# Products of a triangular inverse on 32 columns in place of 64, in one decoder layer on one core

## The chip, the cores and the metric

The kernel runs on one NeuronCore of a Trainium2 chip. The metric is the device time of one execution in microseconds (us); of a set of runs the median is given. Engines are called by the profile's names: PE multiplies matrices (PEld is its loading of weights, the stationary operand), DVE is the vector engine, ACT the scalar engine, POOL the GpSimd engine, SP the queue that issues most transfers.

## What is computed

One layer of a hybrid decoder, on 256 tokens of width 2048, float32 throughout:

```
x = x + 0.5 * swiglu(rmsnorm(x), w1)                       # 2048 -> 5632 -> 2048
z = rmsnorm(x) @ w_in                                      # attention part | RWKV-7 part
x = x + concat(attention(z), rwkv7(z)) @ w_out
x = x + 0.5 * swiglu(rmsnorm(x), w2)
x = x + sigmoid(rmsnorm(x) @ w_ple_gate) * (p @ w_ple_proj)
```

The RWKV-7 part has 16 heads of 64 columns, each with a 64 x 64 state that every token changes:

```
def step(state, inp):
    r_t, w_t, k_t, v_t, kk_t, a_t = inp
    sa = einsum('bhvk,bhk->bhv', state, -kk_t)
    state = state * w_t + sa[..., None] * (kk_t * a_t) + v_t[..., None] * k_t
    return state, einsum('bhvk,bhk->bhv', state, r_t)
```

## The kernel before

The feed-forward parts and the projections stream float32 weights from memory in blocks of 1 MB. ACT rounds a block (L335), DVE takes the rest (L344), and PE forms three products of each tile (L358 to L360). They take the time up to some 1000 us and from 1161 us on.

Between them lies the RWKV stage. It doesn't step through the tokens: the 256 tokens are cut into 4 chunks of 64, and within a chunk the recurrence is one triangular system of 64 unknowns for each head. The 16 heads go in 4 groups (`GROUPS`, index `r`) of 4 heads, so a group has 16 systems. Two systems, of the two chunks in a tile of 128 tokens, stand one above the other on partitions 0 to 63 and 64 to 127; so the tiles `AB` (the systems' matrices), `X` (the inverse so far), `XT` (its transpose) and `Q` have 8 entries `s` of 64 columns, and each entry takes two calls of `matmul`, one for each half of the partitions (`c` in 0, 1). Both calls use a 64 x 64 corner of PE's array, and the two corners lie on its diagonal.

The inverse is built by doubling, in six levels with blocks of l = 1, 2, 4, 8, 16, 32. Level 1 is a predicated copy (L1613). The other five (`INV`, index `n` from 0 to 4) each make two products. The first is AB times XT, into a PSUM bank; ACT copies from it into `Q` the columns that belong to even blocks of l columns (L1493). The second is X times Q (at the last level Q times X), into another bank; DVE takes from it, by `copy_predicated` with a constant mask, the even blocks' columns into `XT` (L1633; at the last level the odd blocks' columns into `X`, L1631), and turns 32 x 32 blocks of `XT` over into `X` (`flip`, L1620). So of each 64-column product only 32 columns are read. `Q`'s other columns are zero from the start.

The 8 entries go in halves `h` of 4, so that ACT and DVE can work on one half while PE works on the other: PE does both halves of the first product, then both of the second, each half waiting on its own semaphore count (`low_ready`, `inv_qs` with `up_ready`). The order of every engine is written out by hand. Between the levels stand other works: on PE the gates of the next group (`pe_gates`, L1247 to L1264) and the transposes of the previous group's output (`pe_out`, L1424); on DVE the next group's preparation (`front`, L1552 to L1582) during levels 2 to 4, the previous group's normalisation (`out_centre`, `out_spread`, L1690 to L1699) in levels 0 and 1, and in the last group splits of weight blocks (L344). POOL ends the normalisation (L1059, L1160), and `pe_out` waits for it. After the inverse the chunk states follow in `pe_state` (L1363 to L1401).

`matmul(out, a, b)` holds `a` in the array and streams `b` through it. In the trace a float32 call leaves two records of loading and two of multiplying, so a half of 8 calls has 16 records and both halves have 32.

Of the kernel before, what the change touches and what calls it, by code (L numbers as in the profile page):

```python
# [16 lines left out]
P = 128  # L17
# [14 lines left out]
CHUNK = 64  # L32
# [85 lines left out]
def hybrid_layer(nc, table, w, out):  # L118
    where = constant_table()[1]
    ctx = ExitStack()  # L120
    with ctx:
# [10 lines left out]
        def sb(name, shape, dt=F32, at=None):  # L132

            if at is None:
                at = base[0]
                base[0] += -(-size(shape) // 64) * 64
                assert base[0] <= limit, (name, base[0] - limit)
            return nc.alloc_sbuf_tensor_at(name, shape, dt, offset=at)
# [21 lines left out]
        def const(name):  # L160
            a, n = where[name]
            return con[:, a:a + n]
# [6 lines left out]
        h = sb("h", [P, TT, COLS])  # L169
# [52 lines left out]
        X = sb("X", [P, 8, CHUNK], at=HT)  # L222
        Q = sb("Q", [P, 8, CHUNK], at=HT + 2048)
        pvst = sb("pvst", [P, TT, COLS], at=HT + 4096)
        XT = sb("XT", [P, 8, CHUNK])
        AB0 = base[0]
        AB = sb("AB", [P, 8, 2 * CHUNK])
# [36 lines left out]
        PS = ctx.enter_context(nc.psum_tensor("PS", [P, 8, COLS], F32))  # L264
        ident = const("ident")

        def sem(name):
            return ctx.enter_context(nc.semaphore(name))
# [34 lines left out]
        low_ready, up_ready = sem("low_ready"), sem("up_ready")  # L303
# [910 lines left out]
        INV = LEVELS[1:]  # L1214
        EARLY, LATER = (0, 1), (2, 3, 4)

        def odd_cols(a, l):

            return a.rearrange("p s (b two l) -> p s b two l", two=2, l=l)[:, :, :, 1, :]

        def even_cols(a, l):
            return a.rearrange("p s (b two l) -> p s b two l", two=2, l=l)[:, :, :, 0, :]

        HALF_BANKS = ((6, 4), (7, 5))
# [3 lines left out]
        def ahead(r, n):  # L1228

            if r == GROUPS - 1:  # L1230
                return ()
            return {2: (0,), 3: (1, 2), 4: (3, 4)}.get(n, ()) if r == 0 else (n + 1,) if n + 1 < GATE_PARTS else ()
# [5 lines left out]
        def pe_gates(pe, r, part):  # L1238

            mine, wl3 = fr(r).sigw, WL[r % 2]  # L1240
            if part == 0:
                if r == 0:
                    pe.wait_ge(ho_ready, 2)
                pe.wait_ge(*loaded(r))
                for k in range(2):
                    for t in range(TT):
                        ins = nc.tensor.matmul(PS[:, gate_bank(r, k), t * 256:(t + 1) * 256], lora_t[0:65, k, t * P:(t + 1) * P],  # L1247
                                               wl3[0:65, k, :], start=True, stop=True)
            for t in range(TT):
                one, two = PS[:, gate_bank(r, 0), t * 256:(t + 1) * 256], PS[:, gate_bank(r, 1), t * 256:(t + 1) * 256]  # L1250
                if part == 1:
                    pe.wait_ge(gates_ready, 2 * r + 1)
                    ins = nc.tensor.matmul(one, const("cum_in"), mine[:, t, :], start=True, stop=True)
                elif part == 2:
                    pe.wait_ge(gates_ready, 2 * r + 2)
                    ins = nc.tensor.matmul(two, const("cum_ex"), mine[:, t, :], start=True, stop=True)
                elif part == 3:
                    pe.wait_ge(exps_ready, 5 * r + 2)
                    for pr in range(2):
                        ins = nc.tensor.matmul(PS[:, gate_bank(r, 0), pr * 4 + 2 * t:pr * 4 + 2 * t + 2],  # L1260
                                               mine[:, t, pr * P:(pr + 1) * P], const("cum_all"), start=True, stop=True)
                elif part == 4:
                    pe.wait_ge(exps_ready, 5 * r + 3)
                    ins = nc.tensor.matmul(two, lora_t[:, 2, t * P:(t + 1) * P], wl3[:, 2, :], start=True, stop=True)  # L1264
            ins.then_inc(lora_out, 1)

        def systems(lo=0, hi=8):

            return [(s, s // 4, (s // 2) % 2, s % 2) for s in range(lo, hi)]
# [18 lines left out]
        def half(k):  # L1288
            return slice(k * CHUNK, (k + 1) * CHUNK)
# [25 lines left out]
        def by_chunks(bank, s, out_col, a, a_cols, b, start=True, stop=True):  # L1315

            for c in range(2):
                ins = nc.tensor.matmul(PS[half(c), bank, out_col:out_col + CHUNK], a[half(c), s, a_cols], b[half(c)],  # L1318
                                       start=start, stop=stop)
            return ins  # L1320

        def pe_inverse(pe, r, levels):

            for n in levels:
                last = n == len(INV) - 1
                for h in range(2):
                    pe.wait_ge(low_ready, 9 * r + (1 if n == 0 else 2 * n + h))
                    for s, *_ in systems(4 * h, 4 * h + 4):
                        ins = by_chunks(HALF_BANKS[h][0], s, (s % 4) * CHUNK, AB, half(0), XT[:, s, :])
                    ins.then_inc(inv_q, 1)  # L1330
                for part in ahead(r, n):
                    pe_gates(pe, r + 1, part)
                for h in range(2):
                    pe.wait_ge(inv_qs, 10 * r + 2 * n + h + 1)
                    pe.wait_ge(up_ready, 11 * r + (1 if n == 0 else 2 * n + h))
                    for s, *_ in systems(4 * h, 4 * h + 4):
                        a, b = (Q, X) if last else (X, Q)
                        ins = by_chunks(HALF_BANKS[h][1], s, (s % 4) * CHUNK, a, half(0), b[:, s, :])
                    ins.then_inc(inv_x, 1)

        def own_tokens(pe, t):
# [146 lines left out]
        def act_inverse(act, r, levels):  # L1488
            for n in levels:
                l = INV[n]  # L1490
                for h in range(2):
                    act.wait_ge(inv_q, 10 * r + 2 * n + h + 1)
                    nc.scalar.activation(even_cols(Q[:, 4 * h:4 * h + 4, :], l),  # L1493
                                         even_cols(PS[:, HALF_BANKS[h][0], 0:256].rearrange("p (s c) -> p s c", s=4), l),
                                         ACT.Copy).then_inc(inv_qs, 1)
                for part in ahead(r, n):
                    act_gates(act, r + 1, part)
                if r == GROUPS - 1 and n in LATER[:2]:
                    act.wait_ge(front_ready, 4 * GROUPS)
                    split_hi(act, WOUT + n - LATER[0])  # L1500
# [45 lines left out]
        def dve_rwkv(dve):  # L1546
            v = nc.vector
# [44 lines left out]
            def joins(l, k, n):  # L1592
                return const(f"join{l}")[:, 32 * k:32 * k + 32].rearrange("p (b l) -> p b l", l=l).unsqueeze(1).broadcast_to(
                    [P, n, 32 // l, l]).bitcast(U32)
# [27 lines left out]
            def inverse(r, levels, nxt, before, heads=False):  # L1622
                for n in levels:
                    l, last = INV[n], n == len(INV) - 1
                    for h in range(2):
                        dve.wait_ge(inv_x, 10 * r + 2 * n + h + 1)
                        v.memset(gate_step[:, h:h + 1], 0.0)
                        src = PS[:, HALF_BANKS[h][1], 0:256].rearrange("p (s c) -> p s c", s=4)
                        mine = slice(4 * h, 4 * h + 4)
                        if last:  # L1630
                            v.copy_predicated(odd_cols(X[:, mine, :], l), joins(l, 0, 4), odd_cols(src, l)).then_inc(up_ready, 1)  # L1631
                        else:
                            v.copy_predicated(even_cols(XT[:, mine, :], l), joins(l, 1, 4), even_cols(src, l)).then_inc(low_ready, 1)  # L1633
                            dve.wait_ge(low_ready, 9 * r + 2 * n + h + 2)
                            flip(X, XT, 4 * h, 4 * h + 4).then_inc(up_ready, 1)
                        if nxt is not None:
                            front(nxt, 2 * (n - LATER[0]) + h)
                        elif n in LATER[:2] and h == 1:
                            dve.wait_ge(front_ready, 4 * GROUPS)
                            split_lo(dve, WOUT + n - LATER[0])  # L1640
                        if heads and h == 1:
                            dve_heads_lo(dve, n)
                        if before is not None and (n, h) == (0, 1):
                            out_centre(before)
                        if before is not None and (n, h) == (1, 1):
                            out_spread(before)
# [327 lines left out]
```

## Time and profile before

| what | value |
|---|---|
| median of 3 runs | 2094.85 us (2089.59 to 2095.48) |
| the profiled execution | 2094.18 us, span 2092.4 us |
| PE busy | 2032.9 us, 97% of the span |
| DVE, ACT, POOL busy | 55%, 41%, 7% |
| mean granted clock of PE | 0.991 of full |
| 996 to 1161 us: PE busy, granted clock | 130.26 of 165 us, 0.92 |

The span goes from the first to the last instruction. A granted clock of 1.00 is PE's upper level, 2.4 GHz, and 0.50 its lower one, 1.2 GHz; a value between them is a mean over a stretch that has both. Busy time counts a matmul from its start to its modelled end, and matmuls overlap, so a busy PE need not be at its peak rate.

### The profile page before, as it was taken

How to read it: one execution, taken by the hardware profiler on the slowest of the kernel's cores; microseconds unless marked ns; L12 is line 12 of the kernel's file. 1: busy time of each engine (PE TensorE's matmuls, PEld its weight loads, DVE VectorE, ACT ScalarE, POOL GpSimd, SP SyncE). 2: the span in 40 equal slices, each digit the busy share in tenths (PEclk: the TensorE clock that was granted, in tenths of full speed). 3: DMA queues.
4: the chain of work that ended last, by engine and by line, in shares of the span. 5: the costliest groups of instructions: out<-in, count | busy, mean ns of one | idle time of the engine just before them, and what ended most of it. 6: DMA issues, size and time to landing. Idle time of an engine off the chain costs nothing.

```text
span 2092.4 us, 27658 instructions
## 1 busy us (share of the span) xinstructions
PE 2032.9 (97%) x11448; PEld 1696.6 (81%) x11448; DVE 1154.4 (55%) x1027; ACT 861.3 (41%) x833; POOL 148.6 (7%) x117
## 2 busy tenths in 40 slices
PE   8999999999999998999787999999999999999999
PEld 6888888888888887888676887888888888888887
DVE  4455545555555554767677444455554555455564
ACT  5343334333433346853332336333333434343353
POOL 0000000000000000354324100000000000000000
PEclk9999999999999999999998999999999999999999
DMA  7555555655556546766301455555565555555554
GB/s 256 192 190 195 186 190 191 192 188 187 194 184 197 183 146 201 215 189 196 100 24 56 138 186 170 188 190 191 185 196 189 192 193 188 187 194 191 191 180 142
DMA packets 190050, 373.62 MB, mean 179 GB/s; under 512 B 7111, under 2 KB 16963, under 8 KB 189981
## 3 DMA queue, kind: packets, MB, share of 16 engines
q1 hardware_dynamic: 186300, 361.47, 53.5%
q0 software_dynamic: 3680, 11.15, 1.8%
q8 instruction: 53, 0.87, 0.2%
q14 instruction: 17, 0.13, 0.0%
HBM read 363.94 MB, written 5.52 MB: 177 GB/s over the span
## 4 chain that ended last, share of the span: by engine, by line
PE 92%; DVE 5%; issue 2%; DMA 1%; ACT 0%; POOL 0%; SPq 0%; DVEq 0%; POOLq 0%
PE PS L358 29%; PE PS L360 29%; PE PS L359 29%; PE PS L415 1%; PE PS L1318 1%; PE PS L379 1%; DVE wlo L344 1%; DVE X L1620 1%; DVE XT L1633 0%; DMA x_resid<-in_x 0%; PE PS L1282 0%; DVE AB L1606 0%; DMA raw<-in_w_q_b 0%; PE PS L1401 0%; DVE AK L1606 0%
## 5 line engine op out<-in xcount | busy, mean ns | idle before, releaser
L344 DVE TENSOR_TENSOR wlo<-raw,whi 128x2048 fp32r<-128x2048 f32 (+1 forms) x338 | 777.7, 2301 | 763.3 <-PE PS L360 759.5
L335 ACT ACTIVATE whi<-raw 128x2048 fp32r<-128x2048 f32 (+1 forms) x338 | 642.9, 1903 | 996.7 <-PE PS L360 986.1
L358 PE MATMUL PS<-whi,xT_hi 128*128 128x512 f32 (+2 forms) x1936 | 753.0, 389 | 0.0
L360 PE MATMUL PS<-whi,xT_lo 128*128 128x512 f32 (+2 forms) x1936 | 748.2, 386 | 0.0
L359 PE MATMUL PS<-wlo,xT_hi 128*128 128x512 f32 (+2 forms) x1936 | 748.0, 386 | 0.0
L360 PEld LDWEIGHTS PS<-whi,xT_lo 128*128 128x128 f32 x1936 | 363.8, 188 | 73.6
L358 PEld LDWEIGHTS PS<-whi,xT_hi 128*128 128x128 f32 x1936 | 364.0, 188 | 72.0 <-issue 0.4
L359 PEld LDWEIGHTS PS<-wlo,xT_hi 128*128 128x128 f32 x1936 | 364.0, 188 | 72.0
L358 PE MATMUL PS<-whi,hT_hi 128*128 128x512 f32 x680 | 264.8, 389 | 2.6 <-DVE wlo L344 2.6
L360 PE MATMUL PS<-whi,hT_lo 128*128 128x512 f32 x680 | 264.6, 389 | 0.0
L359 PE MATMUL PS<-wlo,hT_hi 128*128 128x512 f32 x680 | 264.5, 389 | 0.0
L358 PEld LDWEIGHTS PS<-whi,hT_hi 128*128 128x128 f32 x680 | 127.6, 188 | 29.2 <-issue 2.8
L360 PEld LDWEIGHTS PS<-whi,hT_lo 128*128 128x128 f32 x680 | 127.6, 188 | 26.5
L359 PEld LDWEIGHTS PS<-wlo,hT_hi 128*128 128x128 f32 x680 | 127.6, 188 | 26.5
L550 DVE SCALAR_TENSOR_TENSOR x_resid<-PS,x_resid 128x512 f32<-128x512 f32 x184 | 118.1, 684 | 50.1 <-PE PS L360 50.1
L815 POOL TENSOR_TENSOR rstd<-rstd,con 128x2 f32<-128x2 f32 x6 | 6.3, 1044 | 1615.2 <-DVE rstd L810 1615.2
L1318 PE MATMUL PS<-XT,AB 64*64 64x64 f32 x640 | 28.7, 239 | 19.7 <-DVE XT L1633 14.6
L397 DVE SCALAR_TENSOR_TENSOR xT_lo<-PS,gains,xT_hi 128x256 fp32r<-128x256 f32 x64 | 26.7, 478 | 32.1 <-ACT xT_hi L388 32.0
L1318 PEld LDWEIGHTS PS<-XT,AB 64*64 64x64 f32 x640 | 23.9, 148 | 24.7 <-DVE XT L1633 17.5
L388 ACT ACTIVATE xT_hi<-PS,gains 128x256 fp32r<-128x256 f32 x64 | 25.4, 476 | 37.7 <-PE PS L379 37.7
L535 DVE SCALAR_TENSOR_TENSOR h<-PS,rstd,silu_g 128x512 f32<-128x512 f32 x44 | 30.9, 744 | 0.0
L541 DVE TENSOR_TENSOR hT_lo<-PS,hT_hi 128x1024 fp32r<-128x1024 f32 x20 | 24.5, 1225 | 10.1 <-ACT hT_hi L484 10.1
(329 smaller groups left out, 1117.4 us busy)
## 6 DMA issues: line engine op xcount, KB each, us to landing
raw<-in_w_gate SPq DMA_DIRECT2D x88, 1024.0 KB, 5.1
raw<-in_w_up SPq DMA_DIRECT2D x88, 1024.0 KB, 5.2
raw<-in_w_down SPq DMA_DIRECT2D x88, 1024.0 KB, 5.1
raw<-in_w_in SPq DMA_DIRECT2D x28, 1024.0 KB, 5.7
raw<-in_w_out SPq DMA_DIRECT2D x16, 1024.0 KB, 5.1
raw<-in_w_ple_gate SPq DMA_DIRECT2D x16, 1024.0 KB, 5.2
raw<-in_w_q_b SPq DMA_DIRECT2D x3, 1024.0 KB, 5.3
z_scratch<-zst POOLq DMA_DIRECT2D x6, 512.0 KB, 3.2
```

Of the source, the lines that this page charges most:

```text
L335: nc.scalar.activation(whi[:, n % WHI, 0:wd], raw[:, n % RAW, 0:wd], ACT.Copy).then_inc(hi_ready, 1)
L344: nc.vector.tensor_tensor(wlo[:, n % WLO, 0:wd], raw[:, n % RAW, 0:wd], f32(whi[:, n % WHI, 0:wd]), ALU.subtract).then_inc(lo_ready, 1)
L358: nc.tensor.matmul(acc, a, whi[:, n % WHI, c], start=st, stop=False)
L359: nc.tensor.matmul(acc, a, wlo[:, n % WLO, c], start=False, stop=False)
L360: ins = nc.tensor.matmul(acc, b, whi[:, n % WHI, c], start=False, stop=en)
L379: ins = nc.tensor.transpose(PS[:, turn_bank(k, u), j * SEQ + t * P:j * SEQ + (t + 1) * P], x[:, t, (2 * u + j) * P:(2 * u + j + 1) * P], i ...
L388: ins = nc.scalar.activation(xT_hi[:, kt, :], PS[:, turn_bank(k, u), j * SEQ:(j + 1) * SEQ], ACT.Copy, scale=gains[:, 16 * k + kt:16 * k + ...
L397: ins = nc.vector.scalar_tensor_tensor(xT_lo[:, kt, :], PS[:, turn_bank(k, u), j * SEQ:(j + 1) * SEQ], gains[:, 16 * k + kt:16 * k + kt + ...
L535: ins = nc.vector.scalar_tensor_tensor(h[:, t, :], PS[:, 2 + t, :], rstd[:, 4 * f + t:4 * f + t + 1], silu_g[:, t, :], ALU.mult, ALU.mult)
L541: nc.vector.tensor_tensor((dst or hT_lo)[:, :, :].rearrange("p (b j) s -> p b (j s)", b=2), PS[:, b:b + 2, :], f32((hi or hT_hi)[:, :, :]) ...
L550: ins = nc.vector.scalar_tensor_tensor(x[:, t, j * COLS:(j + 1) * COLS], PS[:, b + t, :], factor, x[:, t, j * COLS:(j + 1) * COLS], ALU.mu ...
L1318: ins = nc.tensor.matmul(PS[half(c), bank, out_col:out_col + CHUNK], a[half(c), s, a_cols], b[half(c)], start=start, stop=stop)
```

## The change

Both products of every level stream only the 32 columns that the level changes. The streamed operand is read through a pattern that takes every other block of l columns (`changed`), and the 32 results of each entry are written side by side, so that the 4 entries of a half fill columns 0 to 127 of the bank in place of 0 to 255. ACT and DVE then read the bank as one contiguous run (`from_blocks`). What they write is as before. The number and the order of instructions on every engine are the same; the streamed shape of the 640 calls (5 levels, 2 products, 4 groups, 16 calls each) goes from 64x64 to 64x32, the stationary operands stay 64 x 64.

```
+        def changed(a, l, odd):
+
+            return a.rearrange("p (b two l) -> p b two l", two=2, l=l)[:, :, odd, :]
+
+        def by_blocks(bank, s, a, b, l, odd=0):
+
+            for c in range(2):
+                ins = nc.tensor.matmul(PS[half(c), bank, (s % 4) * 32:(s % 4 + 1) * 32].rearrange("p (b l) -> p b l", l=l),
+                                       a[half(c), s, half(0)], changed(b[half(c), s, :], l, odd), start=True, stop=True)
+            return ins
+
+        def from_blocks(bank, l):
+            return PS[:, bank, 0:P].rearrange("p (s b l) -> p s b l", s=4, l=l)
...
-                        ins = by_chunks(HALF_BANKS[h][0], s, (s % 4) * CHUNK, AB, half(0), XT[:, s, :])
+                        ins = by_blocks(HALF_BANKS[h][0], s, AB, XT, INV[n])
...
-                        a, b = (Q, X) if last else (X, Q)
-                        ins = by_chunks(HALF_BANKS[h][1], s, (s % 4) * CHUNK, a, half(0), b[:, s, :])
+                        ins = by_blocks(HALF_BANKS[h][1], s, Q, X, INV[n], 1) if last else by_blocks(HALF_BANKS[h][1], s, X, Q, INV[n])
...
-                                         even_cols(PS[:, HALF_BANKS[h][0], 0:256].rearrange("p (s c) -> p s c", s=4), l),
+                                         from_blocks(HALF_BANKS[h][0], l),
...
-                        src = PS[:, HALF_BANKS[h][1], 0:256].rearrange("p (s c) -> p s c", s=4)
+                        src = from_blocks(HALF_BANKS[h][1], l)
...
-                            v.copy_predicated(odd_cols(X[:, mine, :], l), joins(l, 0, 4), odd_cols(src, l)).then_inc(up_ready, 1)
+                            v.copy_predicated(odd_cols(X[:, mine, :], l), joins(l, 0, 4), src).then_inc(up_ready, 1)
...
-                            v.copy_predicated(even_cols(XT[:, mine, :], l), joins(l, 1, 4), even_cols(src, l)).then_inc(low_ready, 1)
+                            v.copy_predicated(even_cols(XT[:, mine, :], l), joins(l, 1, 4), src).then_inc(low_ready, 1)
```

## Rows read from the trace of the kernel before

**Rows 1.** Stages of the span: busy us and records of each engine, granted clock, DMA share.
```profile
core 0: us, PE busy (x) PEld busy (x) DVE busy (x) ACT busy (x) POOL busy (x), PEclk, DMA share, GB/s
0.00:996.00 996.00, 978.87 (x4549) 818.24 (x4550) 548.14 (x409) 439.09 (x450) 86.83 (x77) 1.00 0.60 193
996.00:1161.00 165.00, 130.26 (x2756) 112.89 (x2755) 116.72 (x270) 52.77 (x126) 51.75 (x33) 0.92 0.20 60
```
**Rows 2.** Groups by line and form, 1000 to 1162 us: busy us, mean ns, idle before.
```profile
L1318 PE MATMUL PS<-XT,AB 64*64 64x64 f32 x640 | 28.7, 239 | 19.7 <-DVE XT L1633 14.6 <-DVE XT L1620 4.8
L1318 PE MATMUL PS<-Q,X 64*64 64x64 f32 x512 | 20.3, 233 | 0.0
L1633 DVE COPY_PREDICATED XT<-con,PS 128x128 f32<-128x128 uint32 x32 | 10.5, 327 | 18.0 <-issue 17.9
L1318 PE MATMUL PS<-X,Q 64*64 64x64 f32 x128 | 6.9, 289 | 0.0
L1631 DVE COPY_PREDICATED X<-con,PS 128x128 f32<-128x128 uint32 x8 | 2.4, 294 | 3.1 <-issue 1.8 <-PE PS L1318 1.2
```
**Rows 3.** Waits, 1000 to 1161 us: us in total, times, longest.
```profile
DVE XT L1633 <- issue: 17.9, 13, 4.4
```
**Rows 4.** Timeline of PE at full clock: start, us from first start to last end.
```profile
1086.03 1.10 PE L1300 MATMUL PS<-ART,BT 64*64 64x128 f32 x32 [1.34 <-DVE ART L1599]
1093.52 0.68 PE L1318 MATMUL PS<-XT,AB 64*64 64x64 f32 x16
1093.51 0.54 PEld L1318 LDWEIGHTS PS<-XT,AB 64*64 64x64 f32 x16 [0.22 <-DVE XT L1633]
1098.43 0.97 PEld L1260 LDWEIGHTS PS<-con,sigw 128*128 128x128 f32 x8
1115.94 0.69 PE L1363 MATMUL PS<-X,alpha 64*64 64x64 f32 x32 [1.00 <-DVE X L1631]
```
**Rows 5.** Durations in ns of single records: shortest, median, longest.
```profile
L1300 PE MATMUL PS<-ART,BT x128: 269/269/320, 999.8 to 1128.7; 64*64 64x128 f32 x128
L1318 PEld LDWEIGHTS PS<-XT,AB x640: 129/135/228, 1004.0 to 1148.4; 64*64 64x64 f32 x160
L1318 PE MATMUL PS<-XT,AB x640: 218/218/366, 1004.1 to 1148.5; 64*64 64x64 f32 x160
L1260 PEld LDWEIGHTS PS<-con,sigw x24: 186/192/192, 1026.8 to 1099.2; 128*128 128x128 f32 x24
L1493 ACT ACTIVATE Q<-PS x40: 277/278/294, 1004.8 to 1148.9; 128x128 f32<-128x128 f32 x40
```
**Rows 6.** Timeline of DVE and PE in the third group's first levels.
```profile
1092.28 1.15 PE L1318 MATMUL PS<-Q,X 64*64 64x64 f32 x32
1093.02 0.44 DVE L1633 COPY_PREDICATED XT<-con,PS 128x128 f32<-128x128 uint32 x1 [1.76 <-issue]
1093.49 0.45 DVE L1620 STREAM_TRANSPOSE X<-XT 128x256 f32<-128x256 f32 x1
1093.87 0.44 DVE L1633 COPY_PREDICATED XT<-con,PS 128x128 f32<-128x128 uint32 x1
1096.77 0.29 DVE L1633 COPY_PREDICATED XT<-con,PS 128x128 f32<-128x128 uint32 x1 [0.48 <-issue]
```
**Rows 7.** Timeline: products of the last group at the lower clock.
```profile
1146.88 1.97 PE L1318 MATMUL PS<-XT,AB 64*64 64x64 f32 x32
1148.64 1.92 PE L1318 MATMUL PS<-X,Q 64*64 64x64 f32 x32
```
**Rows 8.** Stretches of the last group, columns as in rows 1.
```profile
1131.00:1142.00 11.00, 8.80 (x241) 7.78 (x241) 9.94 (x29) 4.09 (x10) 3.08 (x3) 1.00 0.01 3
1142.00:1146.00 4.00, 0.84 (x21) 0.71 (x18) 3.93 (x8) 1.75 (x1) 3.92 (x3) 0.90 0.31 61
1146.00:1152.00 6.00, 6.00 (x102) 5.67 (x106) 3.25 (x7) 1.15 (x3) 5.59 (x3) 0.50 0.82 289
```

## Prediction

> **What bounds the kernel now.** I read the stages first [rows 1]. Up to 996 us PE is busy for 978.87 of 996 us, and nothing in that stage changes. The RWKV stage takes 165 us, 8% of the span, with PE busy for 130.26 us and DVE for 116.72: neither is full, the two hand work to each other. All that the change touches lies here, and the stage that follows is bound by PE again, so a microsecond gained on this stage's path should come out whole at the end.
>
> Then the groups by line [rows 2]. The changed products are 640 + 512 + 128 = 1280 records of PE and keep PE busy for 28.7 + 20.3 + 6.9 = 55.9 us. That is no time to be saved: a record is counted to its modelled end, and much of it lies beside other engines' work. What a shorter product could bring at most is the time in which DVE waits for one. Before L1633 DVE was idle for 18.0 us in all, nearly all of it in 13 places where the profile names no releaser but PE's burst had just ended [rows 3]; before L1631 it was idle for 3.1 us, in some 3 places by the same measure. Together 21.1 us. In the opposite direction PE was idle for 19.7 us ahead of the first products, waiting for DVE. So the levels alternate between waiting for PE and waiting for DVE, and the ceiling of this change, were PE's products free, is about 21 us or 1%.
>
> **What one product costs.** The pace of a burst is its length less the last record's duration, over the number of records less one. A half level's 16 records take 0.68 us and end 218 ns after the last start [rows 4, 5]: (0.68 - 0.218) / 15 = 31 ns each. The same burst's 16 loads take 0.54 us with 135 ns for the last: (0.54 - 0.135) / 15 = 27 ns each. Two corners of the array take turns, so a corner gets one load and one multiplication every 54 to 62 ns.
>
> What needs those 54 ns? Two things could, and they happen to be equally long. First, the streaming. With 128 streamed columns and four corners in turn, L1300 goes at (1.10 - 0.269) / 31 = 27 ns a record, so 107 ns a corner for 128 columns, and 54 for 64. Second, the loading of 64 columns of weights. L1260 streams only 2 columns against full 128-column weights, so its pace is that of the loads: (0.97 - 0.192) / 7 = 111 ns each [rows 4, 5]. A load of 128 columns lasts 192 ns and one of 64 lasts 135, which is 57 ns less for 64 columns fewer: half of the 111. So the loading of a 64-column corner takes about 56 ns, whatever streams behind it. L1363, 64 streamed columns in four corners, goes at (0.69 - 0.218) / 31 = 15 ns a record, 61 ns a corner; this excludes that the 27 to 31 ns are a floor on issuing, but both reasons fit it.
>
> The change halves the streaming (54 to 27 ns a corner) and leaves the loading. My step is that the loads then set the pace: 56 ns a corner, with two corners 28 ns a record, where 27 to 31 are needed now.
>
> The Trainium skill (TensorE: Matmul & The Clock Gate, section LDWEIGHTS) gives a load as its columns over 1.2 per ns, whatever the rows; that makes 53 ns for these 64 columns, and it speaks against this change as the rows do. The Trainium skill (TensorEngine Tiling (Array Packing), section Instruction Overhead) also says that a matmul has an overhead of some 60 cycles, so that one column costs as much as 60, by which 32 columns would gain nothing over 64 either. The trace doesn't bear that second rule out: L1363's 15 ns a record lie below 60 cycles at 2.4 GHz, which would be 25 ns. Were it a floor all the same, the pace would go to 25 ns at best, and the sum below would gain about 1 us more.
>
> **The sum, part by part.**
>
> *PE's pace.* Between two bounds: 31 to 28 ns saves 15 x 3 = 45 ns a half burst; 27 to 29 (a load of 56 ns with a little for the change of weights, as L1260 shows 111 where its streaming neighbour L1300 shows 107) costs 15 x 2 = 30 ns. I take nothing, since the loads' own pace is the better measure of what is left, and that is 27 now.
>
> *The last record.* 128 streamed columns make a record of 269 ns, 64 one of 218 [rows 5]: 51 ns for 64 columns, so 26 ns less for 32 fewer. This counts where another engine waits for a burst: twice in a level's chain (ACT, then DVE), in the some 16 places of 40 where DVE waited for PE at all, so 16 x 2 x 0.026 = 0.8 us. Elsewhere DVE's own work covers it (the normalisation and the front between the copies), and it saves nothing. Taken with the pace's small loss on the same bursts I keep 0.3 us.
>
> *ACT's copies.* They read the bank at every second block now and in one run later. Over all levels, from blocks of 2 to blocks of 32 columns, they take 277 to 294 ns [rows 5]: the pattern costs ACT nothing, so its removal brings nothing. 0.
>
> *DVE's copies.* Here the block does matter: 0.44 us with l = 2 and 0.29 us at the next level [rows 6], and at all larger l, since 8 x 0.44 + 24 x 0.29 makes the 10.5 us of all 32 [rows 2]. Either the source in the bank, in pieces of 8 bytes, is slow, and the change mends it; or the destination XT is, and it stays as it is; no row separates them. There are 2 of them in each group, 8 in all, and they are on the path: the transposition of one half and the copy of the other follow at once at 1093.49 and 1093.87, and PE waits. The bounds are 0 and 8 x 0.15 = 1.2 us. The destination's pattern is the same in either case and ACT, which reads the same source pattern at full rate, speaks for DVE's writing as the reason, so I lean to the lower bound, at 0.3 us.
>
> The Trainium skill (SBUF — State Buffer, the note on cachelines) says that PSUM has lines of 8 bytes and that any non-contiguous pattern in PSUM slows matmuls down; DVE isn't spoken of. The rows of ACT show no such cost for reading.
>
> *The streamed operand in pieces.* With l = 2 PE now reads 8 bytes of every 16. No row has such an operand. If each piece cost double, 32 columns would take what 64 do now, so nothing is lost against before; the gain isn't counted anyway. 0.
>
> *Waits and queues.* No wait, instruction or transfer is added or moved. 0.
>
> Sum: -0.3 - 0.3 = -0.6 us. The profiled execution took 2094.18 us; that leads to 2093.6, and since it lay 0.7 us below the median of the runs shown, I forecast 2094.2 us: no change that can be measured. One run and another of the kernel before differ by up to 5.9 us, so about 0.3% (6.3 us) is what can be told from nothing.
>
> **The rivals.**
>
> *A. Streaming sets the pace, and it halves.* If a load in a 64 x 64 corner takes less than L1260 suggests, the pace falls to the 15 ns that L1363 shows. For it: the two reasons for the present pace could not be told apart above, and no row shows loads alone in a corner. Then each burst of 16 saves 15 x 13 = 0.2 us. The chain of a place where DVE waits has one to three bursts in it, take two, and 16 places give 16 x 0.4 = 6.4 us; some of the waits are only 0.4 to 0.5 us long (0.48 in [rows 6]) and can't give it all, the lower clock gives more. With the 0.6 above: 2088 us, faster by 0.3%. The 21 us can't all go, since ACT's copy and two hand-overs stay in each wait. Against it stand the 56 ns of loading in the same corner.
>
> *B. The clock falls for longer.* The granted clock was 0.92 in this stage [rows 1], so 165 x 0.08 / 0.5 = 26 us of it at the lower level of 1.2 GHz. What went before is little work on PE: in the last group it stays at 1.00 through 1131 to 1142 with 241 records, then PE has 21 records in 4 us, and the clock falls, 0.50 from 1146 to 1152 [rows 8]. The changed products keep PE's records and their length in time, but the array streams half the columns in them. Should the chip count that as less work, the clock falls also in levels that hold it now. A product of both halves takes 1.92 to 1.97 us at the lower level and 1.15 without a wait in it at the upper [rows 6, 7], 0.8 us more in 2 us. So each microsecond at the lower level costs 0.4 us where PE is waited for. It decides (over 6.3 us) from 16 us more at the lower level, all of it on the path, or some 22 with part of it hidden. Were the time at that level doubled, 26 us more, with 0.7 of it on the path: 26 x 0.42 x 0.7 = +7.6 us, 2102 us. Against it: only the stretches that are as thinly filled as 1142 to 1146 fell so far, and the records stay as dense in time as they are.
>
> The Trainium skill (TensorE: Matmul & The Clock Gate, on the clock gate) says that the gate goes by how busy PE has recently been, which fits the fall after the idle stretch in [rows 8] and leaves open how half-filled products count.
>
> *C. The products' pace gets worse.* If load and a short multiplication no longer overlap, a corner needs 56 + 27 = 83 ns, 42 ns a record: 15 x 13 ns = 0.2 us more a burst, and the mirror image of rival A, +6 us, 2100 us. L1260 speaks against it: with the load's 107 to 111 ns its short multiplication hardly shows.
>
> **How the numbers follow.** No measurable change (the sum, with all its bounds from -3 to +2 us): 0.64. A: 0.22, of which three quarters come out over the bound, 0.17. B: 0.09, nearly all over it, and C: 0.03, half of it. The last 0.02 are shifts of the clock either way. So faster by over 0.3% 0.18, slower 0.11, within it 0.71. The main case's own range, with the spread of a median, is 2090 to 2098. To leave out no more than 2 in 10 the range must take in the middle of A and go a good part of the way to B and C: 2086.5 to 2100.5 us.
>
> **What the profile after would show.** Right: in a burst of 16 the loads' pace stays at 27 to 29 ns, the records become some 190 ns long, PE's busy time in the products falls only by the shorter ends of at most 80 bursts, 80 x 0.026 = 2 us of the 55.9, and DVE's idle time before L1633 and L1631's counterparts stays near 21 us. Rival A would show paces near 15 ns and that idle time down by 6 us or more; B a clock under 0.88 in this stage; C loads further apart than 35 ns. The copies with l = 2 will read 0.29 or 0.44 us and so settle whose pattern is slow. The forecast is wrong if the load of a corner is shorter than the 56 ns that I drew from full-width loads, or if the clock shifts.

## The result: 0.25% slower, and the clock of PE is where it went

The changed kernel takes 2100.68 us (median of 12 runs, 2097.91 to 2102.1), the kernel before 2094.89 us in 12 runs beside it (2089.59 to 2098.16): a ratio of 1.0025, 95% interval 1.0017 to 1.0034. That is 5.8 us more.

The page of the changed kernel's profiled execution (2101.75 us) gives the span and PE's granted clock in 40 slices of the span, in tenths:

```profile
span 2099.9 us, 27658 instructions
PEclk9999999999999999999787999999999999999999
```

The instructions are as many as before, and the clock has a dent in three slices, which are the RWKV stage. The stage's row answers to [rows 1]. The stage now ends later (PE takes up the streamed weights at 1170.18 us where it did at 1161.10), so a window of 180 us that holds it in both kernels is set beside it; first the changed kernel:

```profile
996.00:1176.00 180.00, 157.00 (x2785) 137.77 (x2784) 118.77 (x277) 54.24 (x126) 55.01 (x35) 0.75 0.19 55
```

and the kernel before:

```profile
996.00:1176.00 180.00, 145.26 (x2823) 125.24 (x2823) 124.34 (x280) 57.42 (x129) 60.35 (x38) 0.92 0.20 61
```

PE is busy for 12 us more in the same 180 us, with fewer records, and its clock is 0.75 in place of 0.92. At full clock such a window has 0 us at the lower level; a mean of 0.75 means 180 x 0.25 / 0.5 = 90 us there, 0.92 means 29 (the clock has two decimals, so each is good to 2 us). So the change added 61 us at 1.2 GHz. Outside the stage the clock did not move: it is 1.00 from 0 to 996 us and again from 1176 us on in both. The 9.1 us by which PE takes up the weights later are 7.5 us at the end of the span (2099.9 for 2092.4 us).

The groups of the changed products and of the copies that wait for them, 1000 to 1170 us, beside [rows 2], and the wait beside [rows 3]:

```profile
L1329 PE MATMUL PS<-XT,AB 64*64 64x32 f32 x640 | 33.1, 259 | 14.0 <-DVE XT L1646 8.9 <-DVE XT L1633 4.8
L1329 PE MATMUL PS<-Q,X 64*64 64x32 f32 x512 | 24.9, 260 | 0.0
L1646 DVE COPY_PREDICATED XT<-con,PS 128x128 f32<-128x128 uint32 x32 | 10.5, 327 | 23.6 <-issue 23.2
L1329 PE MATMUL PS<-X,Q 64*64 64x32 f32 x128 | 7.6, 292 | 0.0
L1644 DVE COPY_PREDICATED X<-con,PS 128x128 f32<-128x128 uint32 x8 | 2.4, 294 | 1.9 <-issue 1.7
...
DVE XT L1646 <- issue: 23.2, 13, 4.9
```

Half the streamed columns, and PE is busy with these products for 65.6 us, not 55.9. DVE waits longer ahead of its copies, 23.6 + 1.9 = 25.5 us for 21.1, and PE waits less for DVE, 14.0 us for 19.7: PE has become the later of the two for more of the time.

At full clock the products are what the prediction said. The third group's first levels, in the timeline of PE, its loads and DVE, beside [rows 4, 6]:

```profile
1099.62 1.12 PE L1329 MATMUL PS<-Q,X 64*64 64x32 f32 x32
1100.33 0.43 DVE L1646 COPY_PREDICATED XT<-con,PS 128x128 f32<-128x128 uint32 x1 [1.70 <-issue]
1100.81 0.54 PEld L1329 LDWEIGHTS PS<-XT,AB 64*64 64x64 f32 x16 [0.19 <-DVE XT L1646]
1100.82 0.65 PE L1329 MATMUL PS<-XT,AB 64*64 64x32 f32 x16
```

The 16 loads still take 0.54 us, so 27 ns each; the burst takes 0.65 us for 0.68, and DVE's wait of 1.76 us before the first copy is now 1.70. So the halved stream saves 0.03 us a burst where the clock is full. In the last group, where no other work of PE stands between the levels, the clock tells the story (timeline of PE, then two stretches as in [rows 8]):

```profile
1142.00 1.91 PE L1329 MATMUL PS<-XT,AB 64*64 64x32 f32 x32
1143.72 1.90 PE L1329 MATMUL PS<-Q,X 64*64 64x32 f32 x32
1145.42 1.90 PE L1329 MATMUL PS<-XT,AB 64*64 64x32 f32 x32
...
1140.00:1144.00 4.00, 3.92 (x101) 3.67 (x99) 3.26 (x10) 0.90 (x4) 0.00 (x0) 0.79 0.01 4
1144.00:1160.00 16.00, 14.12 (x250) 13.65 (x248) 12.93 (x31) 6.09 (x10) 12.87 (x7) 0.50 0.35 114
```

Before, the same levels ran at 1.00 from 1131 to 1142 us and fell only after the 4 us in which PE had 21 records [rows 8]. Now the clock falls at the second level, in the midst of 101 records in 4 us, and stays at 0.50.

### The profile page after: what moved, and what is told of

Its sections match the earlier page's. It is cut to its first block, busy times and chain, and to the rows that moved or that the text cites. A ratio compares the mean times of both kernels' runs of the same rounds, so it can differ in the third digit from the quotient of the medians.

```text
span 2099.9 us, 27658 instructions
## 1 busy us (share of the span) xinstructions
PE 2053.3 (98%) x11448; PEld 1716.8 (82%) x11448; DVE 1152.5 (55%) x1027; ACT 860.9 (41%) x833; POOL 146.7 (7%) x117
## 4 chain that ended last, share of the span: by engine, by line
PE 91%; DVE 5%; issue 2%; DMA 1%; POOL 0%; ACT 0%; SPq 0%; DVEq 0%; POOLq 0%
PE PS L358 28%; PE PS L359 28%; PE PS L360 28%; PE PS L415 1%; PE PS L1318 1%; DVE wlo L344 1%; PE PS L379 1%; DVE X L1633 1%; DVE XT L1646 0%; DMA x_resid<-in_x 0%; PE PS L1282 0%; DMA z_scratch<-zl 0%; PE PS L1329 0%; DVE AB L1619 0%; PE PS L1414 0%
## 5 line engine op out<-in xcount | busy, mean ns | idle before, releaser
L1329 PE MATMUL PS<-XT,AB 64*64 64x32 f32 x640 | 33.1, 259 | 14.0 <-DVE XT L1646 8.9
L1329 PEld LDWEIGHTS PS<-XT,AB 64*64 64x64 f32 x640 | 29.6, 180 | 18.3 <-DVE XT L1646 10.9
```

The source lines that it names most:

```text
L1329: ins = nc.tensor.matmul(PS[half(c), bank, (s % 4) * 32:(s % 4 + 1) * 32].rearrange("p (b l) -> p b l", l=l), a[half(c), s, half(0)], chan ...
```

## The experiments

Theory 1 is rival B of the prediction: with half the columns streamed, PE's clock stays at the lower level for longer. The rivals are that something else in the edit costs the time (the streamed operand in pieces, the results' place in the bank, the readers' pattern), and that it is not the streamed columns but PE's being occupied that holds the clock. "Low clock" in the table is 180 us times (1 less the clock) over 0.5, from the window 996 to 1176 us of each kernel's own profiled execution, which can lie off the median, and is good to 2 us. Ratios are to executions of the kernel before on the same chip; the medians of these were 2093.88 us for the first to fourth kernel, 2094.88 for the fifth to eighth, and 2094.48 for the ninth, the tenth and the second set of the sixth. The expectations count 84 fillers, or 84 and 19. The table `FILL` below adds up to 87, and the traces have 174 records of them, two to a product; with 19 more there are 106, with 212 records.

| kernel | columns | fillers | median us | ratio (95%) | clock 996 to 1176 | low clock us |
|---|---|---|---|---|---|---|
| before | 64 | none | 2094.89 | 1 | 0.92 | 29 |
| changed | 32 | none | 2100.68 | 1.0025 (1.0017 to 1.0034) | 0.75 | 90 |
| first | 64, packed | none | 2093.88 | 1.0007 (0.9997 to 1.0017) | 0.94 | 22 |
| second | 32, spread | none | 2099.91 | 1.0028 (1.0017 to 1.0039) | 0.75 | 90 |
| third | 32 | 87 of 128 | 2097.61 | 1.0018 (1.0009 to 1.0027) | 0.91 | 32 |
| fourth | 64 | 87 of 128 | 2091.07 | 0.9984 (0.9975 to 0.9993) | 0.99 | 4 |
| fifth | 48 | none | 2097.05 | 1.0016 (1.0007 to 1.0024) | 0.83 | 61 |
| sixth, again | 64 | 87 of 2 | 2094.76 | 1.0002 (0.9993 to 1.0011) | 0.92 | 29 |
| seventh | 32 in 4 of 20 levels | none | 2093.12 | 1.0000 (0.9987 to 1.0012) | 0.94 | 22 |
| eighth | 128 | none | 2105.76 | 1.0063 (1.0048 to 1.0078) | 0.98 | 7 |
| ninth | 64, packed | 87 of 128 | 2091.74 | 0.9985 (0.9976 to 0.9994) | 0.99 | 4 |
| tenth | 32 | 106 of 128 | 2095.66 | 1.0005 (0.9996 to 1.0014) | 0.93 | 25 |

**First: 64 columns in the new layout.** PE streams the 32 changed columns and then the other 32; the readers take runs of 32.

```
+                b4 = b[half(c), s, :].rearrange("p (b two l) -> p two b l", two=2, l=l)
...
-                                       a[half(c), s, half(0)], changed(b[half(c), s, :], l, odd), start=True, stop=True)
+                                       a[half(c), s, half(0)], b4, start=True, stop=True)
...
-            return PS[:, bank, 0:P].rearrange("p (s b l) -> p s b l", s=4, l=l)
+            return PS[:, bank, 0:256].rearrange("p (s two b l) -> p s two b l", s=4, two=2, l=l)[:, :, odd]
```

> Streams all 64 columns again, the 32 changed ones first and the other 32 behind them, with the streamed operand still read in alternate blocks; ACT and DVE read runs of 32 contiguous columns per entry. Theory 1 (halving the streamed columns lets PE's clock stay low for longer): the time of the kernel before, 2092 to 2097 us, granted clock over the whole span 0.99, ratio to the kernel before 0.999 to 1.001. Theory 2 (the streamed operand in pieces, or the readers' pattern, costs something by itself): 2099 to 2103 us at a clock near 0.98 or above.

2093.88 us: back at the kernel before, clock too. The alternating blocks in the stream and the changed readers cost nothing that can be measured.

**Second: 32 columns in the old layout.** Only the stream is halved; the results go to every other block as before.

```
-                ins = nc.tensor.matmul(PS[half(c), bank, (s % 4) * 32:(s % 4 + 1) * 32].rearrange("p (b l) -> p b l", l=l),
+                ins = nc.tensor.matmul(changed(PS[half(c), bank, (s % 4) * CHUNK:(s % 4 + 1) * CHUNK], l, odd),
```

> Streams 32 columns as the change does, but PE writes them where they stood before, in alternate blocks of the 64, and ACT and DVE read as before. Theory 1 (the halved stream): as the changed kernel, 2099 to 2103 us, clock 0.975 to 0.98. Theory 2 (packing the results in the bank is what costs): the kernel before's 2092 to 2097 us.

The whole loss is there, with the same clock. Its row:

```profile
996.00:1176.00 180.00, 157.70 (x2786) 138.40 (x2785) 119.20 (x278) 54.23 (x126) 55.71 (x36) 0.75 0.19 55
```

These two leave nothing but the number of streamed columns as the cause of the loss.

**Third: fillers in the changed kernel.** Extra products into columns of PSUM banks that nobody reads, of a constant 128 x 128 matrix with 128 columns streamed. They stand ahead of PE's long waits; they add work and change no result.

```
+        FILL = {(0, 0, "lead"): 8, (0, 3, "mid"): 16, (0, 4, "mid"): 5,
+                  (1, 3, "mid"): 8, (1, 4, "mid"): 5, (1, 4, "end"): 5,
+                  (2, 3, "mid"): 8, (2, 4, "mid"): 8, (2, 4, "end"): 3,
+                  (3, 0, "lead"): 8, (3, 4, "out"): 13}
+
+        def fill(r, n, place):
+            for _ in range(FILL.get((r, n, place), 0)):
+                nc.tensor.matmul(PS[:, {"lead": 2, "mid": 7, "end": 0, "out": 7}[place], 256:384], const("cum_in"), ident[:, 0:P], start=True, stop=True)
```

> The changed kernel with 84 extra 128x128x128 products whose results nobody reads, placed in PE's long waits for DVE and POOL (two before a first level, between the halves of levels 3 and 4, before the wait for the finished inverse, before the last transposes). Theory 1: with the idle stretches filled the clock holds, 0.99 or more over the span; the changed kernel lost about 8 us of stage to the clock, so it comes to 2086 to 2094 us, and within 2 us of the kernel before with the same filling. Theory 2 (the loss is not the clock's): the filling can only cost, 2101 to 2108 us.

A miss for both theories. Low-clock time fell from 90 to 32 us, and on this chip 9 of the 11 executions are faster than all 7 of the second kernel (2097.61 us for 2099.91). But the kernel reached neither the 2094 us of Theory 1 nor the kernel before, and it lies 6.5 us above the fourth kernel, which has the same fillers, where Theory 1 had said 2 us at most. That gap is as large as the one without fillers, though only 28 us of low clock lie between these two, and 61 between the kernels without. The timeline of PE shows one reason:

```profile
1016.22 1.04 PE L1329 MATMUL PS<-XT,AB 64*64 64x32 f32 x16
1017.20 6.11 PE L1343 MATMUL PS<-con 128*128 128x128 f32 x32
1023.23 0.66 PE L1329 MATMUL PS<-XT,AB 64*64 64x32 f32 x16
```

The clock had already fallen in the two levels before, so the 16 fillers, sized for a wait of 4.3 us, took 6.1 and PE came late to the second half.

**Fourth: the same fillers in the kernel before.**

> The kernel before with the same 84 extra products. Theory 1: some 26 us at the lower level go, worth 0.2 to 0.4 us each, so 2085 to 2091 us, less 1 to 3 us given back where the filling is longer than the wait. Rival (the low clock stretches lie where PE is not waited for): 2095 to 2100 us.

2091.07 us, a ratio of 0.9984 (0.9975 to 0.9993): faster than both kernels, as Theory 1 said, though just above its 2085 to 2091 us, for the gain is only 2.8 us. The low-clock time is nearly gone:

```profile
996.00:1176.00 180.00, 160.44 (x3010) 138.94 (x3009) 130.04 (x281) 58.35 (x129) 59.82 (x38) 0.99 0.22 64
...
1014.58 0.68 PE L1318 MATMUL PS<-XT,AB 64*64 64x64 f32 x16
1015.20 3.84 PE L1329 MATMUL PS<-con 128*128 128x128 f32 x32
1020.82 0.68 PE L1318 MATMUL PS<-XT,AB 64*64 64x64 f32 x16 [1.79 <-DVE XT L1645]
```

The same 16 fillers take 3.84 us here, PE still waits 1.79 us behind them, and the next half's products run at full clock (0.68 us, where the kernel before has 1.12 at that place).

**Fifth: 48 columns.** The changed ones and 16 others of each entry.

```
-            return a.rearrange("p (b two l) -> p b two l", two=2, l=l)[:, :, odd, :]
+            w = l + l // 2
+            return a.rearrange("p (b m) -> p b m", m=2 * l)[:, :, (2 * l - w) * odd:(2 * l - w) * odd + w]
```

> Streams 48 columns of each entry, the 32 changed ones and 16 of the others. Theory 1 (the clock goes with how much PE's array streams): between 64 and 32 columns, so low-clock time in the RWKV stage between 27 us (64) and 89 us (32), some 40 to 65, and 2095 to 2099 us. Theory 2 (something else in a stream shorter than 64, all or nothing): at one of the two ends, 2093 to 2095 or 2099 to 2102 us. Both: the pace of a burst stays at 27 to 31 ns a record, since loads set it.

Between the two in time (2097.05 us) and in low-clock time (61 us, in a profiled execution of 2101.82 us, so that of a median one may be lower). So the loss isn't a matter of all or nothing at some width between 32 and 64. The granted clock of the median executions over the whole span says the same: 0.991 with 64 columns, 0.987 with 48, 0.978 with 32.

**Sixth: fillers of 2 columns.** The fourth kernel with its fillers streaming 2 columns against the same full loads.

```
-                nc.tensor.matmul(PS[:, {"lead": 2, "mid": 7, "end": 0, "out": 7}[place], 256:384], const("cum_in"), ident[:, 0:P], start=True, stop=True)
+                nc.tensor.matmul(PS[:, {"lead": 2, "mid": 7, "end": 0, "out": 7}[place], 256:258], const("cum_in"), ident[:, 0:2], start=True, stop=True)
```

> The kernel before with the same 84 extra products as the filled one, but each streams 2 columns against the same full load, so that on PE they take the same time (a record 111 ns for 107). Theory 1 (streamed columns keep the clock up, not records or their time): the clock is as in the kernel before or hardly better, low-clock time 20 us or more, and no gain: 2093 to 2096 us. Rival (PE's being occupied keeps it up): as with 128 columns, under 8 us of low clock, 2089 to 2092 us.

Median 2093.42 us, ratio 1.0000 (0.9988 to 1.0012). Two of its 11 executions were above 2104 us, and the profiled one was one of these (2105.39 us, 44 us at the lower level in its profile), so it was run again:

> The same kernel as the one before with 84 extra products of 2 columns, once more, since its profiled execution (2105 us) was far above its median of 2093.4. Theory 1: median 2092 to 2096 us, ratio to the kernel before 0.999 to 1.001, low-clock time 15 to 45 us. Rival (filling of any width holds the clock): 0.9985 or less and under 8 us.

2094.76 us. Its stage and the same place as above:

```profile
996.00:1176.00 180.00, 166.13 (x2998) 145.96 (x2997) 124.18 (x280) 57.27 (x129) 59.78 (x38) 0.92 0.21 61
...
1014.70 3.73 PE L1329 MATMUL PS<-con 128*128 128x2 f32 x32
1019.05 1.12 PE L1318 MATMUL PS<-XT,AB 64*64 64x64 f32 x16 [0.61 <-DVE XT L1645]
```

PE is occupied for as long (3.73 us for 3.84) and busy for 166 us of the 180, but the clock is the kernel before's 0.92 and the half behind it runs at the lower level, 1.12 us. So in this stage it was not PE's being busy in the records that held the clock, but the columns streamed in that time.

**Seventh: 32 columns only where it is harmless.** In levels 0 and 1 of the second and third group, between which gate products of 256 columns stand; 64 columns elsewhere.

```
+                        ins = by_blocks(HALF_BANKS[h][0], s, AB, XT, INV[n], few=r in (1, 2) and n < 2)
```

> 32 columns only in the first two levels of the second and third group, where gate products of 256 columns stand between and where the changed kernel kept its full clock; 64 columns everywhere else. Theory 1: nothing is lost, low-clock time 15 to 35 us, 2092 to 2096 us. Rival (each 32-column product costs by itself): 8 of 40 half-level pairs are changed, so a fifth of the 6 us loss, 2095 to 2096 us, with an unchanged clock.

2093.12 us, ratio 1.0000 (0.9987 to 1.0012), low clock 22 us: the clock is kept, and no loss can be seen. The interval is 2.6 us wide to either side, so it can tell neither the 0.1 us or so of gain nor the rival's loss of 1.2 us. Against that rival stand the bursts themselves, which at full clock are 0.03 us shorter and not longer.

**Eighth: 128 columns.** Each entry streamed twice over.

```
+                b4 = b[half(c), s, :].unsqueeze(1).broadcast_to([CHUNK, 2, CHUNK])
```

> Streams the 64 columns of each entry twice over, 128 columns. My step that loads and streaming are equally long at 64 says the pace goes to 53 to 55 ns a record, 15 x 26 ns = 0.39 us more a burst of 16. Theory 1: the clock holds better than before, under 15 us at the lower level, but the longer bursts cost 16 waits x 2 x 0.4 = 13 us and more where PE is not waited for now; 2103 to 2112 us. Rival (pace set by loads well above 64 columns): 2090 to 2094 us.

```profile
1050.25 1.96 PE L1330 MATMUL PS<-XT,AB 64*64 64x128 f32 x32 [0.21 <-DVE XT L1635]
```

The clock holds (0.98) and the bursts are bound by streaming: (1.96 - 0.269) / 31 = 55 ns a record, twice the 27. It costs 11 us by the medians, 10 to 16 by the interval of its 5 executions. So at 64 columns streaming and loading take about equally long: of the widths tried, 128 cost time, and 48 and 32 save next to none (0.67 and 0.65 us a burst for 0.68).

**Ninth: the packed layout with fillers.**

> 64 streamed columns with the changed ones packed, and the 84 extra products of 128 columns. Theory 1: the same as the kernel before with the filling, 2089 to 2093 us, under 8 us of low clock in the RWKV stage. Rival (the packed layout has a price that the clock hid): 2 us or more above that.

2091.74 us, ratio 0.9985 (0.9976 to 0.9994), the same as the old layout with fillers. At a held clock too no price of the layout can be seen.

**Tenth: more fillers in the changed kernel.** 19 more, two or three in each level where the clock had still fallen.

```
-        FILL = {(0, 0, "lead"): 8, (0, 3, "mid"): 16, (0, 4, "mid"): 5,
+        FILL = {(0, 0, "lead"): 8, (0, 1, "mid"): 3, (0, 2, "mid"): 3, (0, 3, "mid"): 16, (0, 4, "mid"): 5,
...
```

> The changed kernel with the 84 extra products and 19 more, two or three between the halves of the levels where its clock had still fallen with the first filling. Theory 1: low-clock time under 15 us (34 with the first filling), and since the first filling's own blocking was long only at the low clock, 2090 to 2095 us in place of 2097.6, less what the 19 put on the path, up to 19 x 0.24 = 4.6 us. Rival (the filling itself, not the clock, kept that kernel above the one before): it gets slower, 2098 to 2103 us.

2095.66 us, ratio 1.0005 (0.9996 to 1.0014), 25 us of low clock in a profiled execution of 2098.76 us. The loss against the kernel before is no longer measurable, and the rival, that more fillers make it slower, is out. Its own executions, with the same instructions each time, go with the clock: the four with a granted clock of 0.996 or 0.997 over the span took 2092.5 to 2093.5 us, the five with 0.991 to 0.993 took 2096.9 to 2099.6. But the bound of 15 us was missed in the profiled execution, whose third group still fell, and the kernel is some 4 us slower than the ninth, which has 64 columns and the first 87 of these fillers. Fillers that stand in the path are a price of their own; that price and what is left of the clock's were not separated.

## Why the prediction was wrong

**The forecast** was 2094.2 us and no measurable change. Measured: 2100.68 us, 5.8 us more than the kernel before in the same runs. That is 0.2 us above the stated range, and less than the 0.3% that the prediction took to be measurable; 12 executions of each kernel resolve it. The likeliest case was not the one that came; rival B was, and its sign, a clock under 0.88 in the stage, is in the trace (0.75). The other signs failed with it: PE's busy time in the products rose by 9.7 us and did not fall by 2, and DVE's idle time went to 25.5 us and did not stay near 21.

**PE's pace** was right. Loads of 64 columns set it: 27 ns a record in the loads at 64 and at 32 streamed columns, and (0.65 - 0.219) / 15 = 29 ns in the burst where it had been 31. The 128-column kernel showed the other half of the argument, 55 ns.

**The last record** was wrong. I had its duration fall by 26 ns with 32 columns fewer. It stays: at full clock the 32-column records of the mixed kernel last 219 ns, as 64-column ones do (218).

```profile
L1330 PE MATMUL PS<-XT,AB x128: 219/219/240, 1047.4 to 1094.4; 64*64 64x32 f32 x128
```

Yet a burst is 0.03 us shorter, as much as I had foreseen. That is luck: it comes from the pace, 15 times 2 ns, which I had put at nothing.

**ACT's copies**: 277 to 294 ns again, no change. **DVE's copies**: those with l = 2 still take 0.43 us although their source is contiguous now. So the pieces of 8 bytes in the destination make them slow, or the mask's pattern, which stays too; not the source. The term was 0 and not 0.3 us. **The stream in pieces** cost nothing measurable (first kernel).

**Rival A** (faster by halved streaming) fell with the loads' pace. **Rival C** (worse pace) fell with the same rows.

**Rival B** is where the prediction failed, in its weight and in both its terms. The sum had no term for the clock, and I gave the rival 0.09, with the argument that only stretches "as thinly filled as 1142 to 1146" fell so far and that "the records stay as dense in time as they are". The first half was already wrong in the trace of the kernel before, where the clock fell right behind a stretch that was half full:

```profile
1100.00:1104.00 4.00, 1.97 (x53) 1.70 (x50) 3.34 (x9) 0.35 (x2) 2.52 (x2) 1.00 0.01 4
1104.00:1108.00 4.00, 4.00 (x40) 3.01 (x39) 1.34 (x4) 0.81 (x2) 3.92 (x4) 0.57 0.00 0
```

The 2-column fillers show why the second half doesn't help: dense records with little streamed in them left the clock where it was, while 128-column ones in the same places held it.

I put the added low-clock time at 26 us; it was 61. I put the price of each microsecond at 0.42 x 0.7 = 0.29 us; between the two kernels it was (5.8 + 0.3) / 61 = 0.1 us, with the 0.3 us that I had expected from the last records. Two places show why it is less. In the last group's bare levels a level takes no 2.3 us at full clock, as two products of 1.15 us would make it, for PE waits for DVE in between; first the kernel before, then the changed one at the lower clock:

```profile
1137.34 1.39 PE L1318 MATMUL PS<-XT,AB 64*64 64x64 f32 x32 [0.45 <-DVE XT L1633]
1140.23 1.39 PE L1318 MATMUL PS<-XT,AB 64*64 64x64 f32 x32 [0.45 <-DVE XT L1633]
...
1145.42 1.90 PE L1329 MATMUL PS<-XT,AB 64*64 64x32 f32 x32
1148.84 1.90 PE L1329 MATMUL PS<-XT,AB 64*64 64x32 f32 x32
```

The third level takes 2.89 us at the full clock and 3.42 at the lower one: 0.53 us lost in 3.42, or 0.16 a microsecond. In the first group the third level, with gate products in it, lost as much as I had put for PE being waited for, and the wait behind it gave it back:

```profile
1009.65 1.37 PE L1318 MATMUL PS<-XT,AB 64*64 64x64 f32 x32
1013.95 0.68 PE L1318 MATMUL PS<-XT,AB 64*64 64x64 f32 x16
1018.92 1.12 PE L1318 MATMUL PS<-XT,AB 64*64 64x64 f32 x16 [4.29 <-DVE XT L1633]
...
1011.98 1.92 PE L1329 MATMUL PS<-XT,AB 64*64 64x32 f32 x32 [0.92 <-DVE XT L1646]
1019.26 1.04 PE L1329 MATMUL PS<-XT,AB 64*64 64x32 f32 x16
1021.71 1.06 PE L1329 MATMUL PS<-XT,AB 64*64 64x32 f32 x16 [1.40 <-DVE XT L1646]
```

From 4.30 us that level went to 7.28, 3.0 more (0.41 a microsecond), and the wait for DVE from 4.29 us to 1.40, 2.9 less. The two errors of rival B pull against each other, 7.6 us predicted for the rival and 5.8 measured.

That it was the clock is shown from both sides: removing columns alone brings the loss (second kernel, and in part with 48), putting them back takes it away (first), and holding the clock by other streams takes away a part of it (third, 2.3 us against the second on the same chip) or most of it (tenth) and speeds up the kernel before (fourth), which the same fillers with 2 columns don't do (sixth). How the chip weighs columns, why the clock fell at the second level and not the first, and why the changed kernel stays 6.5 us behind the fourth with the same fillers, stay open.

## What to carry to other kernels

Where small products follow one another on PE between waits, look at what bounds a burst before cutting its columns: if loads already take as long as streaming, fewer columns free no time, and they can lower the clock of everything around them. Read the granted clock of the stretch beside PE's busy share, and ask of every edit that thins PE's streams what holds the clock then. Where the clock falls in a stage of waits, wide products that nobody reads, placed in those waits and shorter than they are, can pay for themselves: 87 of them made the kernel before 0.16% faster (interval 0.07 to 0.25%). A filler that outlasts its wait can give that back: 16 that take 3.84 us at the full clock took 6.11 at the lower one.

## What the runs showed that I had not expected

Fillers with nearly equal time on PE, 3.73 and 3.84 us, differed in the clock by their streamed columns alone, 2 against 128: 0.92 and 0.99 over the 180 us, where the kernel without them has 0.92.

From the kernel before to the changed one a microsecond at half clock cost 0.1 us, though PE is busy for over four fifths of the stage. That is no fixed price. From the fourth kernel to the third, with the same fillers, it is 6.5 us for 28, or 0.23. And among the 29 executions of the kernel before that ran beside the fifth to eighth kernels, whose granted clock over the span went from 0.988 to 0.994, time rose by 0.31 us with each microsecond at the lower clock (correlation 0.96; 0.32 and 0.25 in the other two sets, correlation 0.76 and 0.85). This last is a correlation: what made an execution wait longer may have cost it the clock too.
